# The opening of a two-layer transformer kernel: shift and scale in four quarters on TensorE, x scaled in place, three blocks at once

## The reference, cut to what matters

```python
m_lat = (jax.nn.silu(c) @ mod_w[layer] + mod_b[layer])[:, None, :]
m_ctx = (jax.nn.silu(c_ctx) @ mod_w[layer] + mod_b[layer])[None, None, :]
sh1, sc1, g1, sh2, sc2, g2 = jnp.split(m_lat, 6, axis=-1)
...
u = rms_norm(h, norm_mix_w[layer]) * (1.0 + sc1) + sh1
uc = rms_norm(hc, norm_mix_w[layer]) * (1.0 + csc1) + csh1
...
z = (u @ w_in).astype(jnp.float32)
```

## Time and profile before

| | |
|---|---|
| median of 3 runs | 1705.08 us (1704.41 to 1710.3) |
| span of the profiled execution, first to last instruction | 1703.2 us |
| PE busy in the span | 1652.7 us, 97% |
| DVE busy | 1178.2 us, 69% |
| ACT busy | 891.4 us, 52% |
| POOL busy | 632.6 us, 37% |
| the chain that ended last | PE 68%, DVE 17%, ACT 6%, DMA 3% |
| mean granted clock of TensorE | 0.993 |

### The profile page before, as it was taken

How to read it: one execution, slowest core, us unless ns; L and a number is a source line. 1 busy time by engine, 2 the same in 40 slices (tenths; PEclk the granted TensorE clock), 3 DMA queues, 4 the chain that set the end, 5 groups by cost and what they waited for, 6 DMA issues and landing times.

```text
span 1703.2 us, 27217 instructions
## 1 busy us (share of the span) xinstructions
PE 1652.7 (97%) x10058; PEld 1448.6 (85%) x10058; DVE 1178.2 (69%) x1831; ACT 891.4 (52%) x1520; POOL 632.6 (37%) x368
## 2 busy tenths in 40 slices
PE   7999999998999999999999999999999999999997
PEld 2777888997889999999888888986668989999886
DVE  4779976667888888888757765145774788886114
ACT  3573444776466566555334453214884556776332
POOL 0223124453234444444333423332004256665444
PEclk9999999999999999999999999999999999999999
DMA  8422223343212223333733323364214122332231
GB/s 326 144 99 99 101 97 115 125 133 127 87 56 70 81 94 103 103 103 103 284 125 124 124 98 138 124 210 155 87 57 149 51 87 100 100 99 100 99 99 62
DMA packets 71239, 197.42 MB, mean 116 GB/s; under 512 B 6322, under 2 KB 27186, under 8 KB 69826
## 3 DMA queue, kind: packets, MB, share of 16 engines
q1 hardware_dynamic: 49268, 177.29, 30.1%
q10 hardware_dynamic: 21840, 18.40, 3.5%
HBM read 187.22 MB, written 8.45 MB: 115 GB/s over the span
## 4 chain that ended last, share of the span: by engine, by line
PE 68%; DVE 17%; ACT 6%; DMA 3%; issue 2%; POOL 2%; SPq 0%; ACTq 0%; DVEq 0%; POOLq 0%
PE ps L3723 19%; PE ps L3926 6%; PE ps L3858 6%; PE ps L3260 5%; PE ps L3368 5%; PE ps L3273 3%; PE ps L3259 3%; PE ps L3855 3%; DMA raw<-in_weights 2%; PE ps L4026 2%; PE ps L3673 2%; PE ps L4005 2%; PE ps L4039 2%; DVE conv L2775 2%; PE ps L3374 1%
## 5 line engine op out<-in xcount | busy, mean ns | idle before, releaser
L882 POOL TENSOR_TENSOR wsp<-raw,wsp 128x1024 fp32r<-128x1024 f32 x110 | 287.5, 2614 | 732.4 <-ACT wsp L1034 732.0
L1034 ACT ACTIVATE wsp<-raw 128x1024 fp32r<-128x1024 f32 x110 | 116.7, 1061 | 176.9 <-PE ps L3260 75.2
L3858 PE MATMUL ps<-hsp,wsp 128*128 128x512 f32 x456 | 154.8, 392 | 0.4 <-DVE hsp L2983 0.4
L3723 PE MATMUL ps<-T,wun 128*128 128x384 f32 (+1 forms) x792 | 148.4, 340 | 3.9 <-DVE ps L2156 2.5
L3260 PE MATMUL ps<-u,wsp 128*128 128x512 f32 (+1 forms) x456 | 150.7, 368 | 0.0
L3723 PEld LDWEIGHTS ps<-T,wun 128*128 128x128 f32 x792 | 141.0, 190 | 4.7 <-issue 4.1
L3273 PE MATMUL ps<-wsp,u 128*128 128x512 f32 x576 | 132.7, 390 | 3.8 <-POOL wsp L882 2.8
L3273 PEld LDWEIGHTS ps<-wsp,u 128*128 128x128 f32 x576 | 107.7, 188 | 28.6 <-POOL wsp L882 3.4
L3259 PE MATMUL ps<-u,wsp 128*128 128x256 f32 (+1 forms) x408 | 125.1, 307 | 1.9 <-POOL wsp L882 1.9
L3368 PE MATMUL ps<-u,wsp 128*128 128x512 f32 x384 | 123.0, 402 | 0.0
L3855 PE MATMUL ps<-hsp,wsp 128*128 128x256 f32 x432 | 119.7, 281 | 1.5 <-DVE hsp L2762 1.4
(11 more groups left out here) (411 smaller groups left out, 3844.3 us busy)
## 6 DMA issues: line engine op xcount, KB each, us to landing
raw<-in_weights SPq DMA_DIRECT2D x281, 512.0 KB, 3.4
nab<-in_nabias ACTq DMA_DIRECT2D x32, 256.0 KB, 2.7
start_w<-in_start SPq DMA_DIRECT2D x6, 1024.0 KB, 20.6
hidden_scratch<-hid0a SPq DMA_DIRECT2D x16, 384.0 KB, 4.7
hid0a<-hidden_scratch SPq DMA_DIRECT2D x5, 768.0 KB, 6.9
h<-in_x SPq DMA_DIRECT2D x4, 768.0 KB, 9.8
mD<-rows_scratch ACTq DMA_DIRECT2D x12, 256.0 KB, 4.5
mqs<-rows_scratch ACTq DMA_DIRECT2D x12, 256.0 KB, 5.5
```

The source lines that it names most:

```text
L882: pool.tensor_tensor(w[:, 1, :], raw[:, raw_index(s) % 4, :], w[:, 0, :].bitcast(F32), ALU.subtract)\
L1034: act.activation(split_of(s)[:, 0, :], raw[:, raw_s % 4, :], ACT.Copy).then_inc(*own.one(hi_ready))
L3723: mm = pe.matmul(out, UNIT[x][:, wp, tile(i)], operand[:, i, xp, 0:out.shape[-1]], start=(start and i == 0 and a == 0), stop=(i == KH - 1 ...
L3858: mm = pe.matmul(lat_of(layer, g, mm_), w, hsp[:, kk, xp, LAT], start=one, stop=last, skip_group_check=True)
```

## The change

- Every shift and scale is now made on TensorE. `start_w` holds four quarters `q`; a quarter has the scale and shift of rows 2q and 2q + 1. `quarter_rows(q)` is eight products of 512 columns with a stationary operand of 32 columns (`c_wide`, silu of c in two columns, zeros in 30), whose outputs go to four groups of 32 partitions of one bank. ScalarE copies that bank (`row_taken`), and `quarter_turned(q)` turns it into columns and adds the four groups by the small matrix `fold`. VectorE adds biases in `quarter_columns(q)`.
- `scale_of`, `shift_part`, `scale_part` and their transposes are gone.
- x is multiplied by root in place: `row_scaled(k)`, one VectorE instruction of 768 columns per row. An operand row is then `first_row(k)` on VectorE (two instructions with two scalars), `first_high(k)` on ScalarE (one copy of 768) and `first_low(k)` on VectorE (one subtraction of 768).
- SP loads x first, then weight block 0 and the quarters with weight blocks 1 to 3 between them. Blocks 2 and 3 have split buffers of their own at the start. The modulation tiles 0 to 3 and the constants come later, four of the constants only once all four quarters are turned.
- TensorE runs blocks 0, 1 and 2 side by side, row by row, with the quarters between them, then blocks 3 and 4, the latter in three pieces.
- On ScalarE `evict(2)` and `evict(3)` now stand ahead of `decay_taken(1)`, and `decay_logs((0, 1))` ahead of `decay_taken(3)`.

```diff
 HEADS = 4
 NT_FIRST = 4
-SC_ROWS = 4
...
-    for s in range(S_DOWN0):
+    order = [("w", s) for s in range(N_START)] + [("m", MOD_FIRST + s) for s in range(N_START)]
+    for s in range(N_START, S_DOWN0):
         order += [("w", s)] + ([("m", MOD_FIRST + s)] if s < S_OUT0 else
                                [("m", MOD_FIRST + s - 4)] if S_OUT0 <= s - 4 < S_MIX else [])
...
+            if 2 <= s < N_START:
+                return wsp_start[s - 2]
...
+        spread_rt = ps[:, 5:7, :].rearrange("p b n -> p (b n)")[:, N_CTX:N_CTX + N_TOK]
...
+        def lat_bank(n):
+
+            return ps[:, 6 if n == 2 else n % 2, :]
 
...
+            def load_quarter(q, j):
+                sp.dma_start(start_w[:, q, 4 * j:4 * j + 4, :], start_d[:, q, 4 * j:4 * j + 4, :])\
+                  .then_inc(sc_loaded[2 * (q - 1) + j].sem, 16)
+
+            for j in range(4):
+                load_x(j)
             load(raw_index(0))
-            load_scales(0)
-            load_scales(1)
-            load(raw_index(1))
-            for s in range(2):
-                load(raw_index(s) + 1)
+            for j in range(4):
+                load_first_quarter(j)
+            for q in range(1, START_Q):
+                load(raw_index(q))
+                load_quarter(q, 0)
+                load_quarter(q, 1)
             next_load(4)
-            sp.wait_ge(mod_done.sem, SC_ROWS)
-            sp.wait_ge(start_columns.sem, SC_TURNED)
+            sp.wait_ge(start_columns.sem, q_rows(1))
+            sp.dma_start(reset[:, :, :], reset_d).then_inc(const_loaded.sem, 16)
+            sp.wait_ge(start_columns.sem, START_DONE)
+            sp.dma_start(aup[:, :, :], a_up_d).then_inc(const_loaded.sem, 16)
+            sp.dma_start(sel[:, :, :], consts_d[:, P:2 * P].rearrange("p (a b) -> p a b", a=2)).then_inc(const_loaded.sem, 16)
             sp.dma_start(rope[:, :, :], rope_d).then_inc(const_loaded.sem, 16)
...
+            def row_taken(q):
+
+                act.wait_ge(start_columns.sem, q_rows(q))
+                act.wait_ge(*own.last())
+                act.activation(start_row[:, q % 2, :], ps[:, 3, :], ACT.Copy).then_inc(*own.one(start_rows))
+
+            def first_high(k):
+
+                q = norm[0]
+                act.wait_ge(*q.t_ready.at(k + 1))
+                act.wait_ge(*own.last())
+                act.activation(u[:, k, 0, :], q.nt[:, k % NT_FIRST, :], ACT.Copy).then_inc(*own.one(q.hi_ready.whole))
+
             high(0)
-            act.wait_ge(sh_ready.sem, 1)
-            high_parts(norm[0], shift(0, 0), all_tokens, range(SC_ROWS))
+            row_taken(0)
             high(1)
-            act.wait_ge(start_columns.sem, SC_DONE)
-            act.activation(shrow[0:2, 0:512], ps[0:2, 7, :], ACT.Copy).then_inc(*own.one(start_rows))
-            high_parts(norm[0], shift(0, 0), all_tokens, range(SC_ROWS, KT))
+            first_high(0)
+            first_high(1)
+            row_taken(1)
+            high(2)
+            first_high(2)
+            first_high(3)
+            row_taken(2)
+            first_high(4)
+            first_high(5)
+            high(3)
+            row_taken(3)
+            first_high(6)
+            first_high(7)
...
             evict(0)
             evict(1)
             decay_taken(0)
+            evict(2)
+            evict(3)
             decay_taken(1)
-            evict(2)
             decay_taken(2)
+            decay_logs((0, 1))
             decay_taken(3)
-            decay_logs((0, 1))
-            evict(3)
             rows_evict()
             evict(4)
...
+            def row_scaled(k):
+
+                dve.wait_ge(*own.last())
+                dve.tensor_tensor(h[:, k, :], h[:, k, :], spread_rt, ALU.mult).then_inc(*own.one(rows_scaled))
+
+            def quarter_columns(q):
+
+                dve.wait_ge(start_columns.sem, q_cols(q))
+                dve.wait_ge(*own.last())
+                two = slice(2 * q, 2 * q + 2)
+                for x, bias in ((0, sc_one[:, two]), (1, vec[:, V_MODB + 2 * q:V_MODB + 2 * q + 2])):
+                    dve.tensor_tensor(modm[:, (1 - x) * KT + 2 * q:(1 - x) * KT + 2 * q + 2, :],
+                                      ps[:, 4, 8 * q + 4 * x:8 * q + 4 * x + 4].rearrange("p (k r) -> p k r", r=2),
+                                      bias.unsqueeze(2).to_broadcast([P, 2, 2]), ALU.add).then_inc(*own.one(dve_own))
+                dve.wait_ge(*own.last())
+                dve.tensor_tensor(amod[:, 0, two, :], modm[:, KT + 2 * q:KT + 2 * q + 2, :],
+                                  vec[:, V_NMIX + 2 * q:V_NMIX + 2 * q + 2].unsqueeze(2).to_broadcast([P, 2, 2]),
                                   ALU.mult).then_inc(*own.one(dve_own))
-                raw_row(SC_ROWS)
-                for k in range(SC_ROWS, KT):
-                    if k + 1 < KT:
-                        raw_row(k + 1)
-                    low_row(k)
+
+            def first_row(k):
+
+                dve.wait_ge(*own.last())
+                q = norm[0]
+                for t, r in ((CTX, 1), (LAT, 0)):
+                    dve.tensor_scalar(q.nt[:, k % NT_FIRST, t], h[:, k, t], amod[:, 0, k, r:r + 1], modm[:, k, r:r + 1],
+                                      ALU.mult, ALU.add).then_inc(*own.one(q.t_ready.whole if r == 0 else dve_own))
+
+            def first_low(k):
+
+                q = norm[0]
+                dve.wait_ge(*q.hi_ready.at(k + 1))
+                dve.wait_ge(*own.last())
+                dve.tensor_tensor(u[:, k, 1, :], q.nt[:, k % NT_FIRST, :], u[:, k, 0, :].bitcast(F32), ALU.subtract)\
+                   .then_inc(*own.one(q.lo_ready.whole))
...
+            row_scaled(0)
+            row_scaled(1)
+            quarter_columns(0)
+            first_row(0)
+            first_row(1)
+            row_scaled(2)
+            row_scaled(3)
+            first_low(0)
+            row_scaled(4)
+            first_low(1)
+            for k in (5, 6, 7):
+                row_scaled(k)
+            for q in range(1, START_Q):
+                quarter_columns(q)
+                first_row(2 * q)
+                first_row(2 * q + 1)
+                first_low(2 * q)
+                first_low(2 * q + 1)
...
+            def quarter_rows(q):
+
+                pe.wait_ge(start_rows.sem, CCOL_READY + q)
+                for k in range(KT):
+                    if q == 0 and k % 2 == 0:
+                        pe.wait_ge(sh_loaded[k // 2].sem, 16)
+                    elif q and k % 4 == 0:
+                        pe.wait_ge(sc_loaded[2 * (q - 1) + k // 4].sem, 16)
+                    group = 32 * (k % 4)
+                    mm = pe.matmul(ps[group:group + 32, 3, :], c_wide[:, k, :], start_w[:, q, k, :],
+                                   start=(k < 4), stop=(k >= 4), skip_group_check=True)
+                mm.then_inc(*own.one(start_columns))
+
+            def quarter_turned(q):
+
+                pe.wait_ge(start_rows.sem, CCOL_READY + q + 1)
+                for t in range(4):
+                    mm = pe.matmul(ps[:, 4, 8 * q + 2 * t:8 * q + 2 * t + 2], start_row[:, q % 2, tile(t)], fold[:, :],
+                                   start=True, stop=True, skip_group_check=True)
+                mm.then_inc(*own.one(start_columns))
...
+            quarter_rows(0)
+            quarter_turned(0)
             first_row(0, 0)
-            for k in range(4, KT):
-                scale_part(k)
+            first_row(1, 0)
+            quarter_rows(1)
             first_row(0, 1)
-            first_row(0, 2)
-            pe.wait_ge(start_rows.sem, SCROW_READY)
-            for k in range(KT - SC_ROWS):
-                mm = pe.transpose(ps[:, 4, 2 * k:2 * k + 2], shrow[0:2, tile(k)], ident[0:2, 0:2])
-            mm.then_inc(*own.one(start_columns))
+            quarter_turned(1)
+            first_row(1, 1)
+            first_row(2, 0)
+            first_row(2, 1)
+            for b in range(3):
+                first_row(b, 2)
+            quarter_rows(2)
             first_row(0, 3)
-            for k in range(4):
-                first_row(1, k)
-            for k in range(4, KT):
-                first_row(0, k)
-                first_row(1, k)
+            quarter_turned(2)
+            first_row(1, 3)
+            first_row(2, 3)
+            first_row(0, 4)
+            quarter_rows(3)
+            first_row(1, 4)
+            quarter_turned(3)
+            first_row(2, 4)
+            for b in range(3):
+                first_row(b, 5)
...
+                elif zp == 1:
+                    pe.wait_ge(in_act_took.sem, 3)
+                    pe.wait_ge(in_dve_took.sem, 2)
...
+            for b in range(2):
+                first_row(b, 6)
+                first_row(b, 7)
+            first_row(2, 6)
             pe.wait_ge(const_loaded.sem, 16 * 5)
             pe.wait_ge(in_act_took.sem, 1)
             decay_inputs(0)
+            first_row(2, 7)
+            projection(3, range(KT))
             decay_inputs(1)
-            projection(2)
```

(5 more changed lines are left out.)

207 lines of the change are left out of this document (65 added, 142 removed).

## The result

The changed kernel takes 1721.37 us (median of 4, 1720.28 to 1722.46) against 1704.8 for the kernel before: ratio 1.0089, 95% interval 1.0072 to 1.0106. It is slower by 16.6 us by the two medians and by 15.2 by the ratio. The forecast was slower too, but by 8.1: 1713.2 was expected, and 1721.4 lies above the range of 1703 to 1719. The span of the profiled execution is 1720.6 us (before 1703.2), the mean granted clock 0.986 (before 0.993). One execution of a later kernel (`e8_all_three_fill`, 1807.43 us at a mean granted clock of 0.846) was in a slow state and is left out of that kernel's median and ratio.

What follows compares the result with a forecast made beforehand. TensorE's work at the start, gauged by when `turned(4)` starts on VectorE, bounds the kernel. 86.9 (block 3's end) + 23.4 + 1.5 = 111.8, against 103.67, 8.1 later; 1705.1 + 8.1 = 1713.2 us, range 1703 to 1719.

Steps and rivals of the forecast that it cites:

- the gauge: Time at which `turned(4)` can start on VectorE, 103.67 before; what it gains or loses, the end should too.
- the spread root: TensorE at the start, behind root and reciprocal: 3.1 us at 1.2 GHz, against 1.6 before.
- ScalarE's chain through the log-sigmoids: From block 3's end: `evict(3)`, `high`, `decay_taken(1)` and `(2)`, `decay_logs`, `decay_taken(3)` in series, 15.3 us.
- the gain of the start: First product of block 0 at 37.4, 7.4 us sooner; used up by block 2's end, 78.05 against 78.20.
- The loss of 9.0 us by the decay order: Block 3's end to `turned(4)`: 23.4 us, against 14.4 before, because ScalarE now carries the stretch.
- first product to block 2's end: Three blocks side by side on TensorE with quarters, turns, a decay input, low clock and waits: 40.65 us.
- If it runs at half clock it takes 5.5; I take 2.8, the row: `sums` on TensorE at the start, behind the sum of squares: taken as 2.8 us, ending at 22.65.
- block 3's end to `turned(4)`: 23.4 us of ScalarE's chain, `sel`, `rows_evict` and `evict(4)`, plus 1.5 for `sel` at the low level.
- Hidden within 1 us: Constants issued about 66.5, in at about 72; `modulate(0)` and `decay_inputs(0)` need them at 71 to 76.
- GpSimd's lock: VectorE's `first_row` waits for GpSimd's `low(1)` until 32.95 through shared ports: 1.9 us on everything that follows.
- Rival 1: Not slower: TensorE at 2.4 GHz, VectorE free of the lock, first product at 33.5, time 1705; chance 0.16.
- Rival 3: Faster: from 103.6 new spacing spares VectorE four GpSimd hold-ups, 8 us; 1697 with rival 1's start; chance 0.05.

Runs made afterwards that it cites:

- e8_all_three_fill: Changed kernel with early highs, loads ahead of constants, split decay order, and filler products ahead of `sums` and first product: ratio 0.9977, median 1702.01 us.
- e11_before_fill: Kernel before the change, with two spare products ahead of the first `shift_part`: ratio 1.0003, median 1705.58 us.
- Experiment 4: Changed kernel with only unread filler products added on TensorE, ahead of `sums` and behind `quarter_turned(0)`: ratio 1.0069, median 1717.24 us.
- e1_logs_behind: Changed kernel with `decay_logs((0, 1))` behind `decay_taken(3)` on ScalarE instead of ahead of it: ratio 1.0079, median 1718.71 us.
- e3_highs_early: Changed kernel with `high(1)` ahead of `row_taken(0)` and `high(2)` ahead of `row_taken(1)` on ScalarE: ratio 1.0071, median 1717.71 us.
- e13_order_alone: Changed kernel with only the decay work spread: decay inputs moved into blocks 3 and 4, log-sigmoids split in two: ratio 1.0034, median 1714.62 us.
- e15_all_but_constants: Changed kernel with early highs and the split decay order, but loads and waits for constants left as they were: ratio 1.0025, median 1711.12 us.
- e5_fill: Changed kernel with unread filler products on TensorE, twenty ahead of `sums` and 28 behind `quarter_turned(0)`: ratio 1.0069, median 1717.24 us.
- e12_repeat: Word-for-word second run of `e8_all_three_fill`, all three edits and both sets of fillers: ratio 0.9981, median 1702.56 us.
- e10_fill_sums_only: As `e8_all_three_fill`, with fillers ahead of `sums` but none ahead of the first product: ratio 1.0005, median 1706.01 us.

## Why the prediction was off, step by step

Right: the gauge, and that everything behind it keeps its distance; the spread root at 2.9 (3.1 taken) and quarters of 1.92 with four groups at once (2.0); ScalarE's chain through the log-sigmoids and TensorE's wait of 5 us before `sel`; that the gain of the start is used up again by block 2's end. The loss of 9.0 us by the decay order was the right main term: mending the order gives back 9.4 us alone and 6.3 with the rest mended, by the ratios, and 8.0 and 6.5 on the ruler.

The forecast for `turned(4)` was 111.8, and it came at 121.33. The 9.5 us between them, by the prediction's own terms:

| step | taken | measured | miss |
|---|---|---|---|
| `sums` | 2.8 | 5.3 | +2.5 |
| all else up to the end of quarter 0 | 25.9 | 26.2 | +0.3 |
| quarter 0's end to the first product | 8.7 | 9.3 | +0.6 |
| first product to block 2's end | 40.65 | 42.0 | +1.4 |
| wait ahead of block 3 | 0.3 | 2.2 | +1.9 |
| block 3 | 8.55 | 10.3 | +1.7 |
| block 3's end to `turned(4)` | 24.9 | 26.1 | +1.2 |

**The failed step is the low clock, costed in some places and left out in others.** "If it runs at half clock it takes 5.5; I take 2.8, the row" stood one item ahead of a spread root costed at half clock "after TensorE idled from 9.6 to 19.9". The idle lies ahead of `sums`, so it was `sums` that met the slow rate first. The cause that the prediction gave is not shown either: TensorE ran at that rate from 2.44 on, and in `e11_before_fill` the row that it reasoned from stayed slow (5.89) with 1.22 us of idle ahead of it instead of 5.10. What the changed kernel took away was the work of the earlier trace rows by which the kernel before was at full rate ahead of its `sums`. Block 3 (1.7) and the products at 50.72 had no term for the clock, and `sel` had 1.5 where it needed 2.6. Experiment 4 shows that it is TensorE's rate and not the products: with the idle filled, `sums` takes 2.7, although the printed clock is 1.00 with and without fillers. The stated range did not save the forecast: its upper end held `sums` at half clock (2.7) and quarters of 2.9 (3.6). The first came, the second did not, and the rest of the miss stood in terms that had no room in it.

**"Hidden within 1 us" for the constants was the second.** Their issue was put at 66.5; the whole front was late, so it came at 70.7, and 8.4 us passed from the first issue to the last landing where 5.5 were taken. This cost 1.9 us of waiting more than taken, and the 1.7 of low clock stood behind it. With the wait taken away 2.6 (alone) and 4.4 us (with the rest mended) come back on the ruler; in time nothing clear of the noise does.

**GpSimd's lock was on the wrong instruction.** The prediction let `low(1)` hold up `first_row` for 1.9 us; it caught the tiny `amod` ahead of it for 2.18, and a second time at 48.73, which was not foreseen. Whether a TENSOR_SCALAR is caught stays open: `first_row` started only when `low(1)` had ended.

Rival 1 (not slower) needed TensorE at 2.4 GHz and VectorE free of the lock. `e8_all_three_fill` comes near to that kernel, with the order mended as well, though its quarter 0 still met the low clock. Its first product stands at 37.4, where the rival had 33.5, and it beats the kernel before by 0.2 per cent only: the first product comes at 37.4 instead of 44.8, but the quarters and turns put 8.6 us of TensorE work (three of 1.92, three of 0.95) between the first product and block 2's end. Rival 3 fell: `turned(4)` to `mv` is 68.0 us, with VectorE 64.72 busy (64.75 in the earlier trace rows).

## What to carry to other kernels

When a change empties an engine ahead of a critical step, cost that step at the low clock, each step behind each idle stretch, not only the one where one first thinks of it; spare products in the gap can buy it back, if the products behind them do turn out faster. Look at the time of products whose fast time is known, and not at the printed clock alone. When three blocks run at once, whatever hung on the end of one block moves to the end of all: list every instruction of the other engines that used to lie in the shade of a block, and place it anew, in pieces if it fits nowhere whole. Judge small edits by one ruler in the trace and by many executions, and each by the kernel before as it ran beside it: by medians of different sets the constants seemed worth 2.7 us, by the ratios 0.5.

## What the runs showed of the hardware that was not expected

- An idle stretch of 1.14 us ahead of 50.72, in a stretch that had its own slow start at 40.72, stood ahead of a granted 0.51 over the next 3.4 us. The length of the idle does not decide alone: behind 1.8 us ahead of block 3 (`e1_logs_behind`) the clock between 80 and 90 stayed at 1.00, behind 2.2 it was 0.83 in the changed kernel, `e3_highs_early`, `e13_order_alone` and `e15_all_but_constants`, but in `e5_fill` it stayed at 1.00 behind the same 2.2, and behind 1.14 at 46.80 as well.
- The clock also fell without an idle stretch of note: in `e8_all_three_fill` it was 0.54 between 27 and 30, mostly under quarter 0, which took 3.43 us, with 0.63 us of idle ahead of the spread root. Quarter 0 took 2.89 in `e12_repeat`, the same kernel, and 3.10 in `e10_fill_sums_only`, but 1.92 in `e5_fill`, where the stretch ran at 1.00. The cause stays open.
- The printed clock is 1.00 over the first 25 us of every run here, also where products take twice their time.
- An instruction of four elements per partition waits as long for GpSimd as a large one: 0.16 us of work took 2.18.
